# Latent layers: the first products behind each norm taken from the raw scaled residual, with mean and root applied on VectorE

## The reference, cut to what matters

```python
x = first_block(...)                     # ... return rms_norm(x, g_final)
for l in range(2):
    u = x * (1 + sc1) + sh1              # modulate
    na_q, na_k, na_v, gl_q, ... = split(u @ w_in[l])
    o = concat(neighborhood_attention(na_q, ...), gla(...), gqa(...))
    x = layer_norm(ALPHA * x + g1 * (o @ w_out[l]), ln1_g[l], ln1_b[l])
    u = x * (1 + sc2) + sh2
    a, b = split(u @ w_ffn_in[l], 2)
    x = layer_norm(ALPHA * x + g2 * ((silu(a) * b) @ w_ffn_out[l]), ln2_g[l], ln2_b[l])
```

## Time and profile before

| what | value |
|---|---|
| median of 3 runs | 2479.12 us (2478.7 to 2482.1) |
| the profiled execution | 2482.07 us |
| its span, first to last instruction | 2480.2 us |
| mean granted TensorE clock | 0.941 |
| PE busy | 2114.4 us, 85% |
| DVE, ACT, POOL busy | 529.6, 375.5, 169.8 us |
| HBM read | 660.86 MB |

### The profile page before, as it was taken

How to read it: one execution, slowest core, us unless ns; L and a number is a source line. 1 busy time by engine, 2 the same in 40 slices (tenths; PEclk the granted TensorE clock), 3 DMA queues, 4 the chain that set the end, 5 groups by cost and what they waited for, 6 DMA issues and landing times. The chain is left out here.

```text
span 2480.2 us, 32860 instructions
## 1 busy us (share of the span) xinstructions
PE 2114.4 (85%) x14388; PEld 1456.6 (59%) x14388; DVE 529.6 (21%) x1134; ACT 375.5 (15%) x683; POOL 169.8 (7%) x162
## 2 busy tenths in 40 slices
PE   5998888887688888887888886889899988889997
PEld 2674464554245555654455532766788866468886
DVE  3434432001430200000001102253200024530002
ACT  1121002121120200000001211324200032420000
POOL 0024000000100000000000000125000002510000
PEclk9998998999799999999899997999999998999999
DMA  9459657999999999999999998420444731134450
GB/s 358 161 217 381 265 227 278 415 413 396 411 414 407 413 404 409 415 414 405 403 416 420 390 404 311 123 69 30 140 147 117 171 116 57 47 103 136 148 141 17
DMA packets 245398, 664.03 MB, mean 268 GB/s; under 512 B 20359, under 2 KB 138280, under 8 KB 202952
## 3 DMA queue, kind: packets, MB, share of 16 engines
q1 hardware_dynamic: 245256, 661.93, 70.2%
HBM read 660.86 MB, written 1.05 MB: 267 GB/s over the span
## 5 line engine op out<-in xcount | busy, mean ns | idle before, releaser
L978 PE MATMUL ps<-arena,ring 128*128 128x256 f32 x2368 | 521.1, 382 | 13.2 <-ACT arena L1888 10.1
L978 PEld LDWEIGHTS ps<-arena,ring 128*128 128x128 f32 x2368 | 452.6, 191 | 77.9 <-issue 10.9
L589 PE MATMUL ps<-arena,ring 128*128 128x256 f32 (+2 forms) x1648 | 381.1, 393 | 21.5 <-DMA ring<-in_w_ffn_in 11.4
L589 PEld LDWEIGHTS ps<-arena,ring 128*128 128x128 f32 (+2 forms) x1648 | 302.9, 188 | 104.9 <-issue 25.9
L1314 PE MATMUL ps<-ring,arena 128*32 128x256 f32 x4096 | 267.3, 408 | 95.2 <-DMA ring<-in_w_up 59.3
L1314 PEld LDWEIGHTS ps<-ring,arena 128*32 128x32 f32 x4096 | 128.6, 115 | 219.1 <-DMA ring<-in_w_up 76.7
L1885 ACT ACTIVATE arena<-ps 128x512 f32<-128x512 f32 (+3 forms) x143 | 77.9, 545 | 1037.8 <-PE ps L589 496.1
L1337 PE MATMUL ps<-ring,arena 128*32 128x512 f32 x1024 | 149.0, 709 | 79.1 <-DMA ring<-in_w_down 73.9
L1337 PEld LDWEIGHTS ps<-ring,arena 128*32 128x32 f32 x1024 | 30.1, 120 | 175.0 <-DMA ring<-in_w_down 113.8
L1041 PE MATMUL ps<-arena,ring 128*128 128x256 f32 x512 | 113.6, 383 | 5.0 <-issue 5.0
L2552 POOL TENSOR_TENSOR XC<-XC,arena 128x256 f32<-128x256 f32 x32 | 23.3, 729 | 1327.7 <-ACT XC L1962 1298.8
(11 more groups left out here) (309 smaller groups left out, 1634.9 us busy)
## 6 DMA issues: line engine op xcount, KB each, us to landing
ring<-in_w_gate SPq DMA_DIRECT2D x64, 2048.0 KB, 13.3
ring<-in_w_up SPq DMA_DIRECT2D x64, 2048.0 KB, 14.3
ring<-in_w_down SPq DMA_DIRECT2D x64, 2048.0 KB, 15.1
ring<-in_w_ada SPq DMA_DIRECT2D x36, 2048.0 KB, 11.9
ring<-in_w_ffn_in SPq DMA_DIRECT2D x64, 1024.0 KB, 8.1
ring<-in_w_ffn_out SPq DMA_DIRECT2D x16, 1408.0 KB, 7.1
ring<-in_w_in SPq DMA_DIRECT2D x9, 2048.0 KB, 8.7
ring<-in_w_out SPq DMA_DIRECT2D x6, 2048.0 KB, 7.9
```

Source lines behind the costliest of these rows:

```text
L589: m = mm(o, a, x, start=(k == 0 and r == 0), stop=(k == kt - 1 and last))
L978: m = mm(b, w[:, k, c:c + P], src[:, k, :], start=(k == 0), stop=(k == kt - 1))
```

## The change

Let r be the residual before the norm, mu its mean and s its inverse root, W a weight, g the gain and A, B the modulation's scale and shift with the norm's bias worked in. The next product is W(A(g(r - mu)s) + B). The change computes W(Ag r) on the raw residual, with two more columns in the moving operand: -Ag, whose product times mu takes the mean off, and B, whose product is the shift. `raw` is 8 tiles of 128 x 258. DVE then forms (product + mu x column 256) x s + column 257 from PSUM.

- Which products: `na_q` of both layers (three tiles, `rq0` to `rq2`, now ahead of the gates and first in the layer's part of `stream`), and the first feed-forward pair of both layers (`ra0`, `ra1` for the gate, `rb0`, `rb1` for the value; a bank each, where there were two tiles to a bank). These are 3 + 4 + 3 + 4 = 14 tiles, 112 matmuls. The last norm has no product behind it and stays.
- ACT writes `raw` tile by tile as the residual arrives (`raw_operand`, 8 Copy activations with a scale per partition) and no longer takes the queries out of PSUM. For the RMS norm ACT also does the squares, which DVE did in one instruction (L1869).
- DVE writes the columns ahead of the residual (`raw_columns`) and does the corrections behind `normed` (`raw_queries`: 3 x 3 instructions, 2 each behind the RMS norm; `raw_hidden`: 12 instructions), before `carried`.
- In the mixers, `na_k` takes the place that `na_q` had ahead of levels 6 to 8, and `na_v` comes ahead of the GLA output.

Bank numbers below are those of PSUM (ps0 to ps7); "xN" is N matmuls in a row.

```diff
@@ stream @@
-            stream += part("gl_g", "gl_qkv", "ga_q", "ga_kv", "na_q", "na_k", "na_v", "wo0", "wo1")
+            stream += part("na_q", "gl_g", "gl_qkv", "ga_q", "ga_kv", "na_k", "na_v", "wo0", "wo1")
@@ PE @@
+            def raw_tile(name, w, c, turn, ks=range(KD)):
+                b = ps[place[name][0]] if ks[0] else open_bank(pe, name)
+                for k in ks:
+                    pe.wait_ge(raw_ready, KD * turn + k + 1)
+                    m = mm(b[:, 0:RAW], w[:, k, c:c + P], raw[:, k, :], start=(k == 0), stop=(k == KD - 1))
...
+            def raw_queries(l, mean=None):
+                w = take(f"na_qx{l}")
+                raw_tile(f"rq0x{l}", w, 0, 2 * l, range(4))
+                if mean:
+                    mean(1, KD - 1)
+                raw_tile(f"rq0x{l}", w, 0, 2 * l, range(4, KD))
+                if mean is None:
+                    b = open_bank(pe, "ssf")
+                    for k in range(KD):
+                        pe.wait_ge(csq_ready[X], k + 1)
+                        m = mm(b[:, 0:T], ones, T1[:, T * k:T * k + T], start=(k == 0), stop=(k == KD - 1))
+                    close_bank(m, "ssf")
+                raw_tile(f"rq1x{l}", w, P, 2 * l)
+                if mean:
+                    variance(X, 1, l - 1, f"x{l - 1}", ALL_BANKS)
+                raw_tile(f"rq2x{l}", w, 2 * P, 2 * l)
...
-                whole(na_qk("q", N, bk))
+                whole(na_qk("k", N, bk))
                 for n in range(6, 9):
                     level(n, X, 1 + l, N, GLA_BANKS)
-                whole(na_qk("k", N, bk))
                 head_roots(X, N, bk, 0, 2 * l + 1)
                 head_roots(X, N, bk, 1, 2 * l + 2)
+                whole(na_v(N, bk))
                 gla_out(X, 1 + l, N, bk)
-                whole(na_v(N, bk))
...
+                w = take(f"fi0{N}")
+                raw_tile(f"ra0{N}", w, 0, 2 * l + 1, range(4))
                 mean(0, KD - 1)
+                raw_tile(f"ra0{N}", w, 0, 2 * l + 1, range(4, KD))
+                raw_tile(f"ra1{N}", w, P, 2 * l + 1)
                 variance(X, 0, l, N, ALL_BANKS)
-                for j in range(11):
+                raw_tile(f"rb0{N}", w, T, 2 * l + 1)
+                raw_tile(f"rb1{N}", w, T + P, 2 * l + 1)
+                for j in range(1, 11):
@@ ACT @@
+            def raw_operand(turn, m):
+                act.wait_ge(res_ready[X], KD * turn + m + 1)
+                if m == 0:
+                    act.wait_ge(raw_cols, turn + 1)
+                step(a(raw[:, m, 0:T], xT[:, m, :], ACT.Copy, scale=GA[:, m:m + 1]), raw_ready)
...
+                for i in range(2):
+                    act.wait_ge(raw_gate, 2 * l + i + 1)
+                    step(a(rawt[:, i, :], rawt[:, i, :], ACT.Silu, bias=cc[:, i:i + 1]))
...
+                for m in range(KD):
+                    raw_operand(0, m)
+                    step(a(T1[:, T * m:T * m + T], xT[:, m, :], ACT.Square), csq_ready[X])
@@ DVE @@
-            step(tt(T1.rearrange("p (a b) -> p a b", b=T), xT, xT, ALU.mult), sq_ready)
+            def raw_value(name, i, scale, shift=None):
+                b = read_bank(dve, name)
+                t = rawt[:, i, :]
+                if shift is None:
+                    step(tt(t, b[:, 0:T], scale, ALU.mult))
+                else:
+                    step(stt(out=t, in0=shift, scalar=b[:, T:T + 1], in1=b[:, 0:T], op0=ALU.mult, op1=ALU.add))
+                    step(tt(t, t, scale, ALU.mult))
+                return b, t
+            def raw_queries(l, scale, shift=None):
+                for i in range(3):
+                    b, t = raw_value(f"rq{i}x{l}", i, scale, shift)
+                    step(ts(naq[:, i, :], t, b[:, T + 1:T + 2], 0.125, ALU.add, ALU.mult), frees=f"rq{i}x{l}")
...
                 normed(X, l, 0)
+                raw_hidden(l, N)
                 carried(X, l, 0)
...
                 normed(X, l, 1)
                 if l == 0:
+                    raw_queries(1, rs2, mu)
                     carried(X, l, 1)
```

More of the change, by code:

```diff
@@ L267, in build @@
         nmc, smc = at(1976, 2, 2), at(1980, 2, 2)
+        RAW = T + 2
+        raw = at(9200, KD, RAW)
+        rawt = at(7152, 4, T)
+        GA, cc = at(2000, 8), at(2008, 4)
         ctx_x = [XC[:, :, 0:T], XC[:, :, T:2 * T]]
@@ L995, in latent @@
                         b = open_bank(pe, f"{kind}{j}_{N}")
-                        tile(b[:, 0:T], w, T * x, U, 2 * l + 1 if j + x == 0 else None)
+                        tile(b[:, 0:T], w, T * x, U, 2 * l + 1 if j == 1 and x == 0 else None)
                         close_bank(tile(b[:, T:2 * T], w, T * x + P, U), f"{kind}{j}_{N}")
@@ L1006, in latent @@
                         mean(1, m_ - 1)
-                mean(1, KD - 1)
-                variance(X, 1, l, N, ALL_BANKS)
+                if l == 0:
+                    raw_queries(1, mean)
+                else:
+                    mean(1, KD - 1)
+                    variance(X, 1, l, N, ALL_BANKS)
             return context, latent
@@ L1375, in _ @@
                 combine(GROUPS - 1, r, ALL_BANKS)
-            sums("ssf", T1v, 3)
             for l in range(2):
@@ L1537, in act_moe @@
                 ctx_stage(s)
-            root("ssf")
         def modulated(dve, step, tell, gain, scale, shift, k, src):
@@ L1839, in dve_moe, with added @@
             tell(sel_ready)
-            def added(g, r):
+            def added(g, r, sem=None):
                 b = read_bank(dve, f"cb{g}{r}")
@@ L1977, in centred_squares @@
             def centred_squares(st, l, r, N):
+                if st == X and 2 * l + r < 3:
+                    for m in range(KD):
+                        raw_operand(2 * l + r + 1, m)
                 evac(f"lm{r}{N}", mu, n=T, scale=1.0 / D)
@@ L2132, in latent @@
                     head_roots(X, N, q)
-                na_q(N)
                 na_k(X, l, N)
+                na_v(X, l, N)
                 gla_squares(X, 1 + l)
-                na_v(X, l, N)
                 gla_roots(X, N)
@@ L2169, in latent @@
                 remodulate(X, l, 0)
-                for j in range(11):
+                for i in range(2):
+                    act.wait_ge(raw_gate, 2 * l + i + 1)
+                    step(a(rawt[:, i, :], rawt[:, i, :], ACT.Silu, bias=cc[:, i:i + 1]))
+                tell(sga_ready[X])
+                for j in range(1, 11):
                     if j >= 2:
@@ L2180, in first_modulation @@
             def first_modulation():
-                act.wait_ge(ab_ready[X], 1)
+                for m in range(KD):
+                    raw_operand(0, m)
+                    step(a(T1[:, T * m:T * m + T], xT[:, m, :], ACT.Square), csq_ready[X])
+                b = read_bank(act, "ssf")
+                step(a(rs, b[:, 0:T], ACT.Sqrt, scale=1.0 / D, bias=tb("eps")), frees="ssf")
+                tell(root_ready)
                 for k in range(KD):
@@ L2295, in residual, with ahead_of, raw_columns, raw_hidden @@
                 tell(res_ready[st])
+            def ahead_of(st, l, r):
+                bias = pc(f"ln{r + 1}_b_{l}", 0, 8)
+                ahead, base = (l, 24) if r == 0 else (l + 1, 0)
+                step(ts(A2[st], mod2[:, ahead, base + 8:base + 16, st], 1.0, None, ALU.add))
+                step(tt(B2[st], A2[st], bias, ALU.mult))
+                step(tt(B2[st], B2[st], mod2[:, ahead, base:base + 8, st], ALU.add))
+                step(ts(AB_[st], bias, ALPHA, None, ALU.mult))
+            def raw_columns(l, r):
+                ahead_of(X, l, r)
+                step(tt(GA, A2[X], pc(f"ln{r + 1}_g_{l}", 0, 8), ALU.mult))
+                step(ts(raw[:, :, T], GA, -1.0, None, ALU.mult))
+                step(v.tensor_copy(raw[:, :, T + 1], B2[X]), raw_cols)
+            def raw_value(name, i, scale, shift=None):
[3 more added lines that the diff above has]
+                    step(tt(t, b[:, 0:T], scale, ALU.mult))
+                else:
+                    step(stt(out=t, in0=shift, scalar=b[:, T:T + 1], in1=b[:, 0:T], op0=ALU.mult, op1=ALU.add))
[5 more added lines that the diff above has]
+                    step(ts(naq[:, i, :], t, b[:, T + 1:T + 2], 0.125, ALU.add, ALU.mult), frees=f"rq{i}x{l}")
+            def raw_hidden(l, N):
+                for i in range(2):
+                    b, t = raw_value(f"ra{i}{N}", i, rs2, mu)
+                    step(v.tensor_copy(cc[:, i:i + 1], b[:, T + 1:T + 2]), frees=f"ra{i}{N}")
+                    tell(raw_gate)
+                for i in range(2):
+                    b, t = raw_value(f"rb{i}{N}", 2 + i, rs2, mu)
+                    if i == 0:
+                        dve.wait_ge(sga_ready[X], 11 * l + 1)
+                    step(stt(out=HID[:, i, :], in0=t, scalar=b[:, T + 1:T + 2], in1=rawt[:, i, :], op0=ALU.add, op1=ALU.mult),
+                         frees=f"rb{i}{N}")
+                tell(hj_ready[X])
             def centre(st, l, r):
@@ L2623, in _ @@
                     sp.dma_start(tab[:, 2 * P:2 * P + n_tab3], I["tables3"]).then_inc(s_tab2, 16)
```

(1 more changed line is left out.)

46 lines of the change are left out of this document (28 added, 18 removed).

## The result

| | before | the change |
|---|---|---|
| median of 4 runs, us | 2479.5 (2478.7 to 2482.1) | 2452.61 (2448.07 to 2454.12) |
| ratio, 95% interval | | 0.9889 (0.9877 to 0.9902) |
| the profiled execution (span), us | 2482.07 (2480.2) | 2454.12 (2452.3) |
| mean granted clock | 0.941 | 0.947 |

The change makes the kernel 1.1% faster, 27 us. The forecast was 2448, its own range 2441 to 2456: sign and size are right. The median lies 4.6 us above the forecast; between the two profiled executions the gain is 27.9 us of the 31.0 forecast, 3.1 us short.

What follows compares the result with a forecast made beforehand. PE, busy 85% of the span, was taken as the bound, its waits and low clock as the gain. 10.7 + 9.3 - 1.1 - 3.3 + 7.6 + 7.6 + 2.2 - 2.0 = 31.0 us gave 2448, own range 2441 to 2456.

Steps and rivals of the forecast that it cites:

- The two first norms: First norms of both layers: raw tiles fill PE's waits and the slow clock goes; gain 10.7 us and 9.3 us.
- Start of layer 0: Layer 0's start, to the gates' end: gates 0.2 us later plus 0.9 for a low clock, cost 1.1 us.
- the 0.9 us charged for it: Layer 0's start: allowance for the squares' sum running at the low clock, 0.9 us of at most 3.5.
- Second norm: Layer 0's second norm and layer 1's gates: waits for U (1.6 to 1.8 us) and `gl_g`'s bank (0.8); cost 3.3 us.
- Queries' slot: Mixers of each layer, where the queries stood: 10.6 us leave PE, 7.6 us gained per layer after the new order.
- The wait of 2.7: Inside `na_v`, each layer: PE waits 2.7 us for the bank of the first head root, which DVE reads late.
- The step that failed: Layer 1's levels: 1.99 us stop and some 2.4 of slow clock don't hang on order; half may go, 2.2 us gained.
- the 2.0 in the sum: The new waits inside `na_v` and at layer 1's gates may bring the low clock; 2.0 us charged for all.
- The clock rival: Clock falls at the new waits (first sum, layer 1's gates, `na_v`): 8 us more, 2456; chance 17%.
- The chain rival: Mixers' chain over DVE, ACT and POOL ends the stage; 2 x 7.6 us of queries' time lost, 2463; chance 12%.
- The 258 columns: Raw products: the 258 wide operand loses its pace, each of 112 matmuls twice as long, 48 us more, 2496; chance 3%.
- no effect: Raw tiles late or a bank holds PE at every norm, PE waits as before: within 5 us of 2479; chance 3%.

Runs made afterwards that it cites:

- e1: The changed kernel without the raw feed-forward pair, both first norms as in the kernel before; 2472.92 us, ratio 0.9965 to the kernel before.
- e7: The changed kernel with the edits of e3 and e4, and the variance ahead of `rq1` at layer 0's second norm; 2441.41 us, ratio 0.9848.
- e8: The kernel of e2 with the variance ahead of `rq1` at layer 0's second norm; 2441.15 us, ratio 0.9842 to the kernel before.
- e11: The changed kernel plus 32 tiny matmuls ahead of layer 0's first raw product and 32 ahead of layer 1's `ga_q`; 2445.19 us, ratio 0.985.
- e3: The changed kernel with DVE reading the head roots' banks between the first diagonal blocks, not behind all four; 2449.61 us, ratio 0.9872 to the kernel before.
- e9: The kernel of e7 plus 32 tiny matmuls ahead of layer 0's first raw product and 32 ahead of layer 1's `ga_q`; 2437.78 us, ratio 0.9822.
- e6: The changed kernel plus 32 tiny matmuls (128 instructions with weight loads) ahead of layer 0's first raw product; 2446.69 us in one run.
- e4: The changed kernel with ring slots of `ga_kv` and `na_k` given back later, so no weight load is in flight inside levels 3 to 8; 2448.81 us, ratio 0.9863.
- e5: The changed kernel measured once more, with nothing altered; 2450.46 us, ratio 0.9872 to the kernel before.
- e2: The changed kernel with the mixers' order of the kernel before (levels 6 to 8 ahead of keys, GLA output ahead of values); 2442.6 us, ratio 0.9846.

## Why the prediction was right, and where it was not

- *The two first norms*: 10.7 and 9.3 forecast, 10.6 and 9.1 in the profile, and 9.0 and 9.3 where e1 takes them back. The order of work, the pace of 0.43 us, U's chain under 6.9 us of raw tiles, and the returned clock all held. One reading was off: 3.8 us at 0.59 lose 1.6 us and not 1.8.
- *Start of layer 0*: working and waits held (gates 0.26 us later behind the 2.19 of a late experts' end; 0.2 forecast). The clock did not fall at the sum, so the 0.9 us charged for it was not paid.
- *Second norm*: 3.3 forecast, 3.5 measured, with waits of 1.57 and 0.70. The scalar from PSUM costs nothing: L2391 takes 0.36 us, like the 0.353 of L2323 in the earlier trace rows. The step overlooked a better order, which e7 and e8 show: with the variance ahead of `rq1`, two raw tiles stand behind it and both waits go.
- *Queries' slot, 7.6 in each layer*: the mechanism is right. From the head roots to the rotation 19.7 us were forecast; e11, without a slow clock there, shows 19.78 (1625.19 to 1644.97) and 19.76. The wait of 2.7 was 2.48. In the changed kernel 1.7 us of slow clock come on top in layer 1, part of the 2.0 in the sum.
- *The step that failed*: "Layer 1 now loses 1.99 us inside its levels ... neither hangs on the order, and half may be missing next time: 2.2 more". The stop was taken for chance. It hangs on how many PE instructions stand ahead of it. The change put the queries' 48 records at the start of the layer and the keys' 48 in their old place, so every level moved back by about 100 instructions. So the stop left layer 1 (slot 10.3; 7.6 and 2.2 forecast) and came up in layer 0, where a weight load was now in flight: 3.04 us, with the clock at 0.51 behind it. Layer 0's slot gave 2.2 in place of 7.6, and the stretch ahead of it, with a stop of 1.10 and slow head sums (2.33 us), lost 2.2 more.
- *The total is nearer than its parts, and that is luck.* Those two misses are 7.6 us, and the late experts' end is another 1.4 net. Against them stand gains that nobody forecast: 1.8 us in layer 1 ahead of the slot, where the stop of 0.81 us and its slow head sums are gone, and 1.6 in layer 1's attention, where the granted clock is 0.98 for 0.96; 0.5 each in two more rows, and the 2.0 that the sum charged for a clock whose cost the rows already hold. e11, without the stops in levels 6 to 8, has a median of 2445.19, 3 us under the forecast: right in mechanism there, with the unforeseen gains on top.
- *The clock rival* (2456) was partly right: the low clock came behind the values' wait and behind the unforeseen stop, and not at the first sum nor at layer 1's gates. *The chain rival* (2463) is out: layer 1's slot gave all that was forecast, and with the 2.5 us wait for DVE gone (e3, e9) the rotation and the scores come 2.7 us earlier still. *The 258 columns* and *no effect* are out by the rows.

**Why PE stops.** The runs show that the place of the stop follows the count of instructions (e6, e9, e11), and that it is longer beside a weight load (e4). The traces that were kept show what PE waits for: its own code, which comes by DMA 256 instructions at a time.

Count PE's instructions in a trace in order of time (matmuls, weight loads and semaphore instructions, from 0). The kernel before has 29189, which is 114.0 times 256, and its queue q8 brings 114 packets of 16.4 KB. e9 has 29455, 115.1 times 256, and one packet more:

```profile
q8 instruction: 115, 1.88, 0.3%
```

So q8 brings PE's code. Behind 1524 us PE has 19 stops of 0.4 us or more inside the levels, over all kernels with a profile here. Every one stands at an instruction whose number is 193 or 194 above a multiple of 256, and at every one PE goes on 1.2 to 1.5 us behind the end of a q8 packet. Call such a number a border. In levels 6 to 8, which are 192 records or 384 instructions with their weight loads, the stop of 2 to 3 us comes exactly where two borders lie inside:

| kernel, layer | numbers of levels 6 to 8 | borders inside | stop, us |
|---|---|---|---|
| before, 0 | 20466 to 20849 | 20673 | none |
| before, 1 | 25449 to 25832 | 25537, 25793 | 1.99 |
| the change, 0 | 20565 to 20948 | 20673, 20929 | 3.04 |
| the change, 1 | 25553 to 25936 | 25793 | none |
| e6, 0 | 20693 to 21076 | 20929 | none |
| e6, 1 | 25681 to 26064 | 25793, 26049 | 3.04 |
| e9, 0 | 20693 to 21076 | 20929 | none |
| e9, 1 | 25809 to 26192 | 26049 | none |

PE runs from the first border to the second in 1.33 us. The packet starts 0.9 to 1.1 us behind the first border with idle DMA queues (before, e4, e7) and 1.8 to 2.0 us behind it beside a weight load (the change, e5, e3, e1, e6); it takes 1.0 to 1.3 us either way. So PE goes on 3.3 to 3.7 us behind the first border in the one case and 4.3 to 4.4 us in the other: the load delays the packet's start. In e2, whose levels 6 to 8 stand near the old numbers, PE waits 2.1 us for GpSimd between the two borders of layer 1; they are 3.5 us apart, and there is no stop.

The Trainium skill, "Advanced Engine Details and Errata", section "ISA Cache", speaks of cache lines of 16 KB, 256 instructions, and of only two of them; it also gives TensorE 128 KB, which would be eight such lines. The packet size agrees. A next block that is there only 3.3 us or more behind the last border is what two lines would give, and not what eight filled ahead would. How many lines PE holds was not tried.

Open: when the packet starts in level 5, where it comes 2.1 to 3.3 us behind the border beside a load and the stop takes 0.8 to 1.8 us, and what sets the experts' end, which moves the gates' start between 1536 and 1548 us.

## What to carry to other kernels

Work that needs only a raw operand belongs under a norm's chain, and its place is counted out tile by tile: here two tiles behind the variance hide all of it, one does not. When an instruction run is moved, ask also what else moves with it: a bank's reader, the start of a weight load, and the block boundaries in the code. A stop marked "issue" inside hundreds of tiny matmuls need not be chance: count the engine's instructions up to it and look for a packet of the instruction queue just ahead of its end, or insert a few instructions ahead of it and see whether it walks. Judge an order only with such stops out of the way, and count what the inserted instructions cost: 32 tiny matmuls took 2.2 us in e9.

## What the runs showed of the hardware that was not expected

- A stop of PE with no semaphore, 2.0 to 2.4 us with idle DMA queues and 3.0 to 3.1 beside a weight load, at a place that 128 added instructions moved from layer 0 to layer 1. All 19 such stops in the levels, from 0.4 us up, stand 193 or 194 instructions above a multiple of 256 and end 1.2 to 1.5 us behind a packet of PE's instruction queue.
- The clock after it: 0.51 over 10.5 us in the changed kernel. Head roots and `na_v` took 4.63 and 12.71 us, against 2.50 and 10.59 in e3's layer 1: 4.3 us lost, more than the stop itself.
- Two layers of the same program can be alike to 0.01 us over 30 us once these are gone.
